# Inner norms: the last three weight chunks token tile by token tile, and the next unit begun on the first tile

## The reference, cut to what matters

```
def rmsnorm(x, g):
    y = x * lax.rsqrt(jnp.mean(x * x, axis=-1, keepdims=True) + RMS_EPS)
    return y * g

for i in range(DEPTH):
    h = rmsnorm(x, g[0]);  mix = attention(h)
    x = x + rmsnorm(mix, g[1])
    h = rmsnorm(x, g[2])
    x = x + rmsnorm(conv_ffn(h), g[3])
```

## Time and profile before

| | |
|---|---|
| median of 3 runs | 2125.11 us (2124.90 to 2125.21) |
| profiled execution | 2124.99 us, its span 2123.3 us |
| TensorE busy | 2111.3 us, 99% |
| VectorE, ScalarE, GpSimd busy | 63%, 50%, 13% |
| granted TensorE clock, mean | 0.999 |
| DMA | 381.42 MB, 180 GB/s |

### The profile page before, as it was taken

One profiled execution on the slowest core, in us unless ns is written; L12 is line 12 of the kernel. 1 busy time (PEld: TensorE's weight loads), 2 busy tenths in 40 slices (PEclk: granted clock), 3 DMA queues, 4 the chain that ended last, 5 costly groups with the idle time before them and its releaser, 6 DMA issues.

```text
span 2123.3 us, 34632 instructions
## 1 busy us (share of the span) xinstructions
PE 2111.3 (99%) x12195; PEld 1808.7 (85%) x12195; DVE 1335.1 (63%) x2031; ACT 1064.3 (50%) x1620; POOL 277.6 (13%) x461
## 2 busy tenths in 40 slices
PE   9999999999999999999999999999999999999999
PEld 9987788888888888888999977888888888888887
DVE  7665676766767754445866664676766767754444
ACT  6675554444444444444656775554444444444443
POOL 4452000000000000001205763000000000000000
PEclk9999999999999999999999999999999999999999
DMA  7444555565565565555673333556555565565553
GB/s 255 150 162 156 169 177 198 179 193 182 178 200 185 185 211 189 188 188 169 217 249 113 106 114 120 168 177 196 180 191 185 177 200 186 182 214 189 188 189 129
DMA packets 107505, 381.42 MB, mean 180 GB/s; under 512 B 14147, under 2 KB 14867, under 8 KB 106771
## 3 DMA queue, kind: packets, MB, share of 16 engines
q1 hardware_dynamic: 105106, 373.63, 53.7%
q10 hardware_dynamic: 2304, 6.53, 0.9%
HBM read 377.97 MB, written 2.14 MB: 179 GB/s over the span
## 4 chain that ended last, share of the span: by engine, by line
PE 98%; DVE 1%; POOL 0%; issue 0%; ACT 0%; DMA 0%; DVEq 0%; ACTq 0%; POOLq 0%
PE set L733 32%; PE set L826 31%; PE set L737 16%; PE set L951 11%; PE set L1025 1%; PE set L999 1%; PE set L1047 1%; PE set L877 1%; PE set L1001 0%; PE set L1049 0%; DVE x_sb L1920 0%; PE set L1115 0%; PE set L1116 0%; POOL probs L671 0%; PE set L1058 0%
## 5 line engine op out<-in xcount | busy, mean ns | idle before, releaser
L1732 DVE TENSOR_TENSOR wlo<-raw,whi 128x1024 fp32r<-128x1024 f32 x703 | 860.4, 1233 | 572.8 <-ACT whi L1285 570.5
L1285 ACT ACTIVATE whi<-raw 128x1024 fp32r<-128x1024 f32 x703 | 737.3, 1056 | 731.2 <-PE set L737 350.6
L733 PE MATMUL set<-hs,whi 128*128 128x512 f32 x2932 | 966.3, 395 | 0.9 <-ACT whi L1381 0.9
L737 PE MATMUL set<-hs,wlo 128*128 128x256 f32 x2944 | 695.5, 281 | 0.0
L737 PEld LDWEIGHTS set<-hs,wlo 128*128 128x128 f32 x2944 | 544.7, 188 | 60.6
L733 PEld LDWEIGHTS set<-hs,whi 128*128 128x128 f32 x2932 | 503.3, 189 | 71.0 <-DVE hs L1822 1.1
L826 PE MATMUL set<-whi,hid 128*128 128x512 f32 x1408 | 388.7, 395 | 0.0
L826 PEld LDWEIGHTS set<-whi,hid 128*128 128x128 f32 x1408 | 264.2, 188 | 64.2 <-DVE wlo L1732 0.6
L826 PE MATMUL set<-wlo,hid 128*128 128x512 f32 x704 | 223.6, 395 | 0.0
L951 PE MATMUL set<-hs,whi 128*128 128x256 f32 x1280 | 213.1, 286 | 0.0
L951 PEld LDWEIGHTS set<-hs,whi 128*128 128x128 f32 x1280 | 176.7, 189 | 2.3 <-issue 0.4
(11 more groups left out here) (208 smaller groups left out, 1346.7 us busy)
## 6 DMA issues: line engine op xcount, KB each, us to landing
raw<-in_stream SPq DMA_DIRECT2D x703, 512.0 KB, 3.5
gain_rows<-rows ACTq DMA_DIRECT2D x4, 1024.0 KB, 5.3
xT<-in_x SPq DMA_DIRECT2D x8, 256.0 KB, 7.7
out_y<-out_f SPq DMA_DIRECT2D x3, 512.0 KB, 3.0
bo_rows<-rows ACTq DMA_DIRECT2D x1, 1024.0 KB, 12.7
wg_raw<-in_w_gates ACTq DMA_DIRECT2D x1, 768.0 KB, 5.2
raw<-in_stream SPq DMA_DIRECT2D x2, 256.0 KB, 4.1
w2k_sb<-in_w ACTq DMA_DIRECT2D x2, 128.0 KB, 7.5
```

The costliest lines, as they stand in the source:

```text
L733: return mm(sets[set_of(u)][:, t, 0:2 * w], whi[:, slot, cols], r, start=first, stop=final)
L737: return mm(sets[set_of(u)][:, t, w:2 * w], wlo[:, slot, cols], r[:, 0:w], start=False, stop=False)
L1285: A(whi[:, slot, :], raw[:, slot, :], ACT.Copy).then_inc(hi_ready, 1)
L1732: V.tensor_tensor(wlo[:, slot, :], raw[:, slot, :], whi[:, slot, :].bitcast(F32), ALU.subtract).then_inc(lo_ready, 1)
```

## The change

The last three chunks of the token unit ahead of an inner norm run tile by tile: all 18 products of tile 0, then all 18 of tile 1, and a chunk's slot is given free by tile 1. Inside tile 1's last chunk TensorE turns tile 0's part of x's first two chunks. The new unit starts with the products of tile 0's tokens, high weights only, over the four (three in the first norm) k-tiles of its first two chunks; then come tile 1's turns and products, the low weights, and from chunk 2 on the old order. The filler products are gone. Semaphores by half become semaphores by part. Only one chunk of the new unit is split ahead of the norm instead of three; the splits of chunks 1 and 2 stand in the norm, and the split of chunk c + 1 stands behind the high part of chunk c. Squares of x and sums of x are spread otherwise. The last norm keeps its order under the name `last_norm`.

TensorE, the token unit and the first chunks:

```
+            def last_chunks(u, k, source, n, between):
+                for t in range(TT):
+                    for c in range(n - HELD, n):               # HELD = 3
+                        g = first_chunk(u) + c
+                        if t == 0:
+                            pe.wait_ge(lo_ready, g + 1)
+                        for j in range(CK):
+                            between(t, c - n, j)
+                            ... three products of tile t ...
+                        if t == 0 and c == n - 1:
+                            ins.then_inc(y_first, 1)
+                        if t == 1:
+                            ins.then_inc(chunk_used, 1)
+            def between_norm(n):
+                def between(t, c, j):
+                    if (t, c, j) == (1, -1, 0):
+                        turn_part(n, 0, 0)
+                    if (t, c, j) == (1, -1, 1 if n == 1 else 0):
+                        turn_part(n, 1, 0)
-            def keep_busy(k):
-                for _ in range(IDLE_PRODUCTS[k]):
-                    mm(sets[1][:, UT - 1, 0:P], ones[:], ident[:], start=True, stop=True)
+            def first_chunks(n, u):
+                early = PARTS[:3] if n == 1 else PARTS        # (0,0), (0,1), (1,0), (1,1)
+                first_tokens((0, 1, 2))                       # tile 0, high weights, waits h_part
+                if n < 3:
+                    first_tokens((3,))
+                turn_part(n, 0, 1)
+                for j in range(CK):
+                    pe.wait_ge(h_part, part_count(n, 0, j, 1))
+                    for tile in range(UT):
+                        if n == 3 and (j, tile) == (0, 3):
+                            first_tokens((3,))
+                        high(0, j, tile, 1)
+                    if j == 0:
+                        turn_part(n, 1, 1)
+                pe.wait_ge(lo_ready, g + 1)
+                ... eight low products, chunk_used ...
+                turn_x(n, CK)
+                ... the same for chunk 1 of tile 1, its low products behind lo_ready, chunk_used ...
```

ScalarE:

```
             def prenorm(n, gain, u):
                 g0 = first_chunk(u)
-                for c in range(CH):
+                split(g0 + 1)
+                for c, kt in PARTS[:3]:
+                    high_of_part(n, gain, c, kt, 0)
+                if n > 1:
+                    high_of_part(n, gain, 1, 1, 0)
+                y_evac(u - 1, n - 1, 3, (1,))()
+                if n == 1:
+                    act.wait_ge(h_part, part_count(n, 1, 0, 0))
+                    high_of_part(n, gain, 1, 1, 0)
+                for c, kt in PARTS:
+                    high_of_part(n, gain, c, kt, 1)
+                split(g0 + 2)
+                for c in range(CK, CH):
                     high_of_h(n, gain, c)
-                    if 1 <= c <= 5:
-                        split(g0 + c + RING - 2)
-                    if 2 <= c <= 5:
+                    if c <= 6:
+                        split(g0 + c + 1)
+                    if c <= 5:
                         square_x(n, c - 2)
                     if c == 6:
                         take_root(n)
-                for c in range(done, n + (0 if last else RING - 1)):
+                for c in range(done, n + (0 if last else 1 if norm_next else RING - 1)):
```

The last line stands on VectorE too. `square_x(n, q)` waits for x up to chunk 2q + 1. VectorE:

```
+            def norms(n, u_last, gain, u):
+                if biased:                                   # the first inner norm
+                    bias_y(u_last, n, 3, 0)
+                inverse_of_y(n, 0)
+                for c in range(CK):
+                    add_y(c, c + 1, x_part, 1, (0,))
+                scale_y(u_last, n, 3, 0)
+                add_y(2, 4, None, 0, (0,))
+                for c, kt in PARTS[:2]:
+                    low_of_part(n + 1, gain, c, kt, 0)
+                if biased:
+                    bias_y(u_last, n, 3, 1)
+                for c, kt in PARTS[2:3] if biased else PARTS[2:]:
+                    low_of_part(n + 1, gain, c, kt, 0)
+                inverse_of_y(n, 1)
+                for c in range(CK):
+                    add_y(c, c + 1, x_part, 1, (1,))
+                if biased:
+                    low_of_part(n + 1, gain, 1, 1, 0)
+                scale_y(u_last, n, 3, 1)
+                ... low_of_part of tile 1 for chunk 0; add_y(2, 3) of tile 1; low_of_part for chunk 1 ...
+                split(g0 + 1);  low_of_h(n + 1, gain, 2);  add_y(3, 4, x_ready, 1, (1,))
+                split(g0 + 2);  low_of_h(n + 1, gain, 3);  add_y(4, 5, x_ready, 1)
                 split(g0 + 3)
+                add_y(5, 6, x_ready, 1);  low_of_h(n + 1, gain, 4)
                 split(g0 + 4)
+                add_y(6, 7, x_ready, 1);  low_of_h(n + 1, gain, 5)
                 split(g0 + 5)
+                add_y(7, 8, x_ready, 1);  low_of_h(n + 1, gain, 6)
                 split(g0 + 6)
+                token_sum(sq_x, x_squared, 8 * (n + 2))
                 split(g0 + 7)
                 token_inverse(n + 1);  make_diag();  low_of_h(n + 1, gain, 7)
```

More of the change, by code:

```diff
@@ L789, in chunk, with unit @@
                 last.then_inc(chunk_used, 1)
-            def unit(u, source, lp=None, width=S, waits=None, tile_before=None, after_chunk=None, spread=0, low_ready=0):
+            def unit(u, source, lp=None, width=S, waits=None, tile_before=None, after_chunk=None, spread=0, done=0):
                 n = CH
@@ L796, in unit @@
                 at = None if v is None else more_e + (UT * v + 1)
-                for c in range(n):
+                for c in range(done, n):
                     g0 = first_chunk(u) + c
@@ L830, in token_chunk, with token_unit @@
                 ins.then_inc(chunk_used, 1)
-            def token_unit(u, k, source, waits=None):
-                for c in range(CHF if source is hid else CH):
+            def token_unit(u, k, source, waits=None, between=None):
+                n = CHF if source is hid else CH
+                for c in range(n - HELD if between else n):
                     if waits:
@@ L878, in turn_x, with turn_part @@
                 ins.then_inc(x_turned, 1)
+            def turn_part(n, c, t):
+                pe.wait_ge(x_part, 4 * (n - 1) + CK * t + c + 1)
+                for kt in range(CK):
+                    ins = nc.tensor.transpose(turned_part(n, c, kt, t), x_sb[:, c, t, kt * P:(kt + 1) * P],
+                                              ident[:])
+                ins.then_inc(x_part_turned, 1)
+            def between_norm(n):
[4 more added lines that the diff above has]
+                        turn_part(n, 1, 0)
+                return between
             def h_waits(n):
                 def waits(c):
[L883 to L885 removed]
                     if n == 0 and c == 0:
@@ L1214, in _ @@
                 else:
-                    turn_x(n, 0)
-                    unit(KC1, hs, waits=h_waits(n), tile_before=mid_chunk(n), low_ready=n)
+                    first_chunks(n, KC1)
+                    unit(KC1, hs, waits=h_waits(n), done=CK)
                     spread_r(n)
@@ L1233, in _ @@
                 output_pair(o0, o_waits, attention(layer, GROUPS - 1))
+                n = 2 * layer + 1
                 for k in range(2, 4):
-                    token_unit(o0 + k, k, os_)
-                n = 2 * layer + 1
-                turn_x(n, 0)
-                unit(ff, hs, waits=h_waits(n), tile_before=mid_chunk(n), low_ready=n)
+                    token_unit(o0 + k, k, os_, between=between_norm(n) if k == 3 else None)
+                first_chunks(n, ff)
+                unit(ff, hs, waits=h_waits(n), done=CK)
                 spread_r(n)
@@ L1951, in norms, with add_y, last_norm @@
+            def add_y(lo, hi, done, by, tiles=(0, 1)):
+                for t in tiles:
+                    ins = V.scalar_tensor_tensor(x_sb[:, lo:hi, t, :], y[:, lo:hi, t, :], r_token[:, t:t + 1],
+                                                 x_sb[:, lo:hi, t, :], ALU.mult, ALU.add)
+                if done is not None:
+                    ins.then_inc(done, by)
+            def last_norm(n, u_last):
+                dve.wait_ge(evacuated, UT * u_last + CK)
                 for t in range(TT):
```

266 lines of the change are left out of this document (142 added, 124 removed).

## The result

The changed kernel takes 2130.47 us in the median of 11 runs (2128.99 to 2132.15) against 2125.11 us before (11 runs, one of which took 4194.83 us; without it the median is 2125.0). The ratio is 1.0028, with a 95% interval of 1.002 to 1.0037: slower by 0.28%, which is little but clear of the noise. The profiled execution has 2131.45 us and a span of 2129.7, 6.4 above that of before.

A forecast was written before the change was run, and what follows sets the result against it. TensorE, busy 99% of the span, bounds the kernel. Its waits at the three inner norms add 5.0 us and one clock fall 1.2: 2124.99 + 5.0 + 1.2 = 2131.2, as median 2131.3, range 2123.5 to 2134.5.

The forecast's parts named there:

- the loop at chunk 6: Chunk 6 of each new unit: its weight split waits behind squares and low part; waits 1.8, 2.0 and 1.8 us.
- Tile 0 hidden, the first wait gone: At an inner norm's start, tile 0's chain finishes before its transposes; first waits of 4.1, 2.8, 2.6 us gone.
- Tile 1 is late next, 3.3 us behind the end: After the old unit's end, tile 1's chain holds TensorE until 3.3 (third norm); waits 2.7, 1.4, 1.7 us.
- the two waits that follow ahead of chunk 2: Third norm, before chunk 2: TensorE waits 0.5 us for the sum of chunk 3 and 0.8 for a split.
- A product over two runs of 128 columns costs 0.117 us: Tile 0's products, 256 columns over two separate runs of 128: not below today's 0.117 us; no extra cost taken.
- The 4 us kept for it: Range allowance should those products be slower, at most 1.3 us a norm; up to 4 us, none in the forecast.
- The front wins 1.7 us, less 0.6 for hand-overs: Old unit's end to chunk 2, all three norms: 1.7 us won; 0.6 us added for hand-overs on longer chains.
- GpSimd's share at the second norm: Second norm: the wait at chunk 6 is 2.0 us beside GpSimd, against 1.8 at the others.
- The clock: one fall, 1.2 us: First inner norm, fillers gone: one fall of the clock from 2.4 to 1.2 GHz, 1.2 us.
- (b): Rival: the weights keep up and only the front counts: 2123.3, or 2124.5 with a clock fall; chance 0.17.
- (c): Rival: tile 0's products cover tile 1's chain, and the loop is hidden too: 2117.4; chance 0.11.
- (d): Rival: the held chunks' own splits come late and stall tile 0, 1.4 us at each norm: 2135.5; chance 0.05.

The follow-up runs named there:

- the scaling's move: Changed kernel with x's last squares behind the copy of chunk 6, first-norm fillers, and scaling of y's last quarter behind tile 1's first low part: 2125.23 us.
- VectorE's swap: Changed kernel with the split of chunk 6 put ahead of the low part of chunk 6 on VectorE: 2126.89 us, ratio 1.0009.
- the late squares: Changed kernel with the squares of x's last quarter moved behind the copy of chunk 6 on ScalarE: 2126.41 us, again 2125.14.
- the best version here: Changed kernel, two chunks held instead of three, the late squares, first-norm fillers, y's last-quarter scaling behind tile 1's first low part: 2123.73 us, ratio 0.9996.

## Why the prediction was right

Forecast 2131.3 us, measured 2130.47. The mechanism that makes most of the loss, the loop at chunk 6, was forecast and shown. By the prediction's steps:

- *Tile 0 hidden, the first wait gone.* Right: TensorE goes on at 249.65, 1000.20 and 1370.23. At the first norm it waits 0.27 us for the third part (0.5 forecast).
- *Tile 1 is late next, 3.3 us behind the end.* Right: 1373.50 - 1370.23 = 3.27 at the third norm. The reason was half right: I named VectorE's queue, and the scaling's move shows that chain and queue end together at the second and third norm. Of the two waits that follow ahead of chunk 2, forecast at 0.5 and 0.8 us, the third norm has 0.35 and 0.57.
- *A product over two runs of 128 columns costs 0.117 us.* Right: twelve of them in 1.59 us, (1.59 - 0.28)/11 = 0.119. The 4 us kept for it weren't needed.
- *The front wins 1.7 us, less 0.6 for hand-overs.* Somewhat too high. From the old unit's end to chunk 2 it is 10.22 + 0.44 at the second norm and 9.99 + 0.44 at the third against 10.86 and 10.55, and 10.67 + 0.6 against 11.81 at the first (the changed kernel's second profile, without a fall): 0.2, 0.1 and 0.5, 0.8 in all against 1.1.
- *The loop at chunk 6.* Right in place, releaser and size: done at T + 8.10 for 8.2 forecast, 1.70, 1.71 and 1.72 us for 1.8, 2.0 and 1.8. GpSimd's share at the second norm doesn't show. Chunks 2 to 5 lose 0.14, 0.24 and 0.15 us against the pace of 3.23, for 0.1, 0.3 and 0.1. The loop is 5.1 us of the loss, taken out by two separate moves: 2.9 to 3.6 us with VectorE's swap, 3.4 to 4.9 with ScalarE's move.
- *The clock: one fall, 1.2 us.* The place was right in the profile, and a fall costs 1.5. It doesn't come in each execution: by the clock of the runs there are 0.74 falls more per run than in the kernel before (1.33 against 0.59), which at 1.5 us are 1.1. So the term comes out near its 1.2, a rarer fall at a higher price; that all of it lies at the first norm isn't shown. The sum without falls is 4.7 over the norms (31.34 + 0.6 - 30.67 = 1.3, then 1.7 and 1.7), 5.0 forecast; with 1.1 it is 5.8, and the medians differ by 5.4 and in the third session by 4.7. The profiles differ by 6.4, 6.2 forecast: both have the fall near 1295 us, and the changed kernel's has one more. The rule of the Trainium skill in "TensorE: Matmul & The Clock Gate", Part 4, that transposes don't count as busy as products do, isn't settled by this: with transposes alone in its waits the clock fell in half of the profiles, with products there in none of six, which agrees with it but would follow from the missing products too.
- *The rivals.* (b), a supply that keeps up, is what the late squares make of the kernel: 2125.14 and 2126.41, where I gave 2123.3 to 2124.5; its price took the front's win at 1.7 us. (c) needed a tile 1 ready within 1.9 us of the end; in the changed kernel its first products come 4.4, 3.4 and 3.3 us behind it, and in no version sooner than 3.3. (d) didn't come: there is no wait inside the held chunks.

So the change gains under 1 us at the front, loses 5.1 by a side effect of the rewritten order and some 0.5 more in the chunks ahead of it, and pays, by the estimate above, about 1 for the falls of the clock. What stays open is how large the effect of the clock is on the median, where the added falls lie, and whether the best version here is faster than the kernel before: its interval includes no change.

## What to carry to other kernels

When a lead of prepared work is given up, look for circles over two engines that each work off their instructions in the order written: write down, from one start of the bound engine to its next need, each hand-over in turn with its traced duration. The shares (63% and 50% busy) showed slack, and two idle brackets of 2 us inside the stall were the sign that order, not load, bound it; moving one line confirmed it. A side computation that nobody needs soon (squares for a later norm) belongs behind the copy that the next chunk waits for. And an idle bracket in front of a group of products is not the whole of what it lost: compare the starts with the undisturbed pace.

## What the runs showed of the hardware

The same kernel's clock fell behind the same waits (0.61 and 1.08 us with two transposes between) in some executions and not in others: at the first norm in one of two profiles of the changed kernel. At L1132 (L1058 before), where TensorE always waits 1.9 us, the clock granted over 1288 to 1308 us was 0.91 in seven of the fourteen profiles and 1.00 in the other seven. Such a fall costs 1.5 us where no wait behind it takes up the slower products, and 0.6 to 0.8 in the kernel before without fillers, where some do. Fillers in the waits make falls rarer: no run of the 30 with fillers at the first norm in the table had two, and 18 of the 40 without had. With none to two falls in a run, this alone moves an execution by up to 3 us, which is likely why differences under 1 us weren't resolved by 11 runs.
